# Other byte offsets for TensorE's two operands: split weights at 144 and 16 modulo 256, the stream as a run of high and a run of low halves

## What is computed

```python
qkv = xn @ w_qkv                      # 2048 x 6144
...
    return o.reshape(b, s, A_V_WIDTH) @ w_o
...
def _conv_ffn(xn, w_up, conv_w, conv_b, w_down):
    up = xn @ w_up                    # 2048 x 11264
    ...
    return (jax.nn.silu(g) * u) @ w_down
...
kv = _rmsnorm(h, kv_norm_g) @ b_w_kv  # 2048 x 4096
```

## Time and profile before

| what | value |
|---|---|
| runs | 2692.2, 2692.35, 2693.52 us |
| median | 2692.35 us |
| profiled execution, its own time | 2691.99 us |
| its span (first to last instruction) | 2689.8 us |
| TensorE (PE) busy | 2679.5 us |
| VectorE (DVE) busy | 1977.5 us |
| ScalarE (ACT) busy | 1197.8 us |
| data moved | 528.18 MB, 196 GB/s |

### The profile page before, as it was taken

One profiled execution on the slowest core, in us unless ns is written; L12 is line 12 of the kernel. 1 busy time (PEld: TensorE's weight loads), 2 busy tenths in 40 slices (PEclk: granted clock), 3 DMA queues, 4 the chain that ended last, 5 costly groups with the idle time before them and its releaser, 6 DMA issues.

```text
span 2689.8 us, 44167 instructions
## 1 busy us (share of the span) xinstructions
PE 2679.5 (100%) x15336; PEld 2348.9 (87%) x15336; DVE 1977.5 (74%) x2594; ACT 1197.8 (45%) x1533; POOL 5.7 (0%) x12
## 2 busy tenths in 40 slices
PE   9999999999999999999999999999999999999999
PEld 7888888888888888888888888888888888888888
DVE  6747577777777788667787776699878876688865
ACT  2004354555555444444444443366544444444443
POOL 0000000000000000000000000000000000000000
PEclk9999999999999999999999999999999999999999
DMA  9986665555556666666666666644566666666664
GB/s 342 366 278 191 205 192 191 165 174 163 160 164 196 188 195 190 198 190 195 189 194 188 196 200 190 188 157 140 181 188 195 196 191 192 192 190 195 196 202 155
DMA packets 705780, 528.18 MB, mean 196 GB/s; under 512 B 32221, under 2 KB 694559, under 8 KB 705439
## 3 DMA queue, kind: packets, MB, share of 16 engines
q1 hardware_dynamic: 701872, 523.73, 63.9%
q10 hardware_dynamic: 3823, 3.31, 0.4%
HBM read 523.80 MB, written 2.10 MB: 196 GB/s over the span
## 4 chain that ended last, share of the span: by engine, by line
PE 97%; DVE 2%; ACT 1%; issue 0%; DMA 0%; DVEq 0%; SPq 0%; ACTq 0%
PE acc L707 80%; PE acc L845 3%; PE acc L1039 2%; PE acc L833 2%; PE turned L845 2%; PE sums L845 2%; PE mixed L960 1%; PE sums L1191 1%; DVE pro_ada L1915 0%; DVE wr L1841 0%; PE scores L1184 0%; PE sums L745 0%; PE mixed L961 0%; PE sums L916 0%; PE scores L946 0%
## 5 line engine op out<-in xcount | busy, mean ns | idle before, releaser
L707 PE MATMUL acc<-stream,wr 128*128 128x512 f32 (+1 forms) x7680 | 1328.4, 333 | 0.3 <-DVE wr L1841 0.3
L707 PEld LDWEIGHTS acc<-stream,wr 128*128 128x128 f32 x7680 | 1159.1, 188 | 156.0 <-issue 3.8
L1841 DVE TENSOR_TENSOR wr<-raw,wr 128x1024 fp32r<-128x1024 f32 x832 | 998.5, 1222 | 318.2 <-ACT wr L1367 308.6
L1367 ACT ACTIVATE wr<-raw 128x1024 fp32r<-128x1024 f32 x832 | 871.1, 1058 | 693.8 <-PE acc L707 678.1
L707 PE MATMUL acc<-ys,wr 128*128 128x512 f32 (+1 forms) x4264 | 732.4, 332 | 1.0 <-DVE wr L1841 0.9
L707 PEld LDWEIGHTS acc<-ys,wr 128*128 128x128 f32 x4264 | 642.7, 188 | 85.3 <-DVE wr L1841 1.5
L707 PE MATMUL acc<-wr,stream 128*128 128x512 f32 (+1 forms) x1024 | 182.7, 338 | 0.0
L707 PEld LDWEIGHTS acc<-wr,stream 128*128 128x128 f32 x1024 | 157.0, 188 | 22.5 <-issue 0.5
L1725 ACT ACTIVATE ffn_cv<-ffn_cv 128x256 f32<-128x256 f32 x88 | 36.9, 419 | 245.4 <-DVE ffn_cv L2459 245.4
L1851 DVE TENSOR_REDUCE ffn_ug<-acc 128x512 f32<-128x1024 f32 x88 | 107.8, 1225 | 35.3 <-PE acc L707 35.3
L1874 DVE TENSOR_TENSOR ys<-tmp,ys 128x256 f32 (+3 forms) x108 | 51.2, 474 | 76.0 <-ACT ys L1373 73.4
(11 more groups left out here) (334 smaller groups left out, 1546.1 us busy)
## 6 DMA issues: line engine op xcount, KB each, us to landing
raw<-in_ffn_w_up SPq DMA_DIRECT2D x704, 256.0 KB
raw<-in_ffn_w_down SPq DMA_DIRECT2D x160, 512.0 KB
raw<-in_a_w_qkv SPq DMA_DIRECT2D x96, 512.0 KB
raw<-in_b_w_kv SPq DMA_DIRECT2D x64, 512.0 KB
aring<-in_w_ada SPq DMA_DIRECT2D x96, 256.0 KB, 6.6
w<-in_w_in SPq DMA_DIRECT2D x48, 512.0 KB
raw<-in_w_ada SPq DMA_DIRECT2D x32, 512.0 KB, 5.1
raw<-in_w_out SPq DMA_DIRECT2D x32, 512.0 KB
```

Of the source, the lines that this page charges most:

```text
L707: mm = pe.matmul(*ops, start=first and ops is wide, stop=last and ops is wide)
L1367: f(half_of(0, s), raw[:, s, :], ACT.Copy)\
L1841: tt(half_of(1, s), raw[:, s, :], half_of(0, s), ALU.subtract).then_inc(T.unit_split[s].sem, 1)
```

## The change

Three layouts are changed; no instruction is added, removed or moved.

- `wr`: WEIGHTS_SHIFT goes from 4 to 36 elements and HALF_PAIR from 2100 to 2080. The highs lie at 144 and the lows at 144 + 8320 = 16 modulo 256. SLOT_PAIR stays 4224 elements.
- `stream`: no longer high and low side by side tile for tile. All 16 high halves form one run, at 80 modulo 256, and all 16 low halves another, LOWS_SHIFT = 96 bytes further modulo 256, at 176. The tile is 192 bytes longer, so what is allocated behind it (`ssq`, `rx`, `kpe`, `ones_r`, `tri_r` and others) moves by 192 bytes.
- `ys` keeps its layout, high and low both at 80; only its view gains a dimension for the half.

All other lines of the diff are that extra dimension: `xs[:, k, :]` becomes `xs[:, k, :, :]`, and a range of columns becomes an index of the half.

```diff
-HALF_PAIR = 2 * UK * 256 + 52
-WEIGHTS_SHIFT = 4
-SLOT_PAIR = -(-2 * HALF_PAIR // 64) * 64
+LOWS_SHIFT = 96
+HALF_PAIR = 2 * UK * 256 + 32
+WEIGHTS_SHIFT = 36
+SLOT_PAIR = -(-(WEIGHTS_SHIFT + 2 * HALF_PAIR) // 64) * 64
...
-        stream = sb("stream", [KT * 2 * TOK + 2 * MOVING_SHIFT // 4], F32R)
-        xs_at = nc.sbuf_base - KT * 2 * TOK * 4 - 2 * MOVING_SHIFT
...
-        xs = moving_tiles(stream, KT)
+        run = KT * TOK + LOWS_SHIFT // 4
+        stream = sb("stream", [2 * run + 2 * MOVING_SHIFT // 4], F32R)
+        xs_at = nc.sbuf_base - 2 * run * 4 - 2 * MOVING_SHIFT
+
+
+        xs = stream[:, MOVING_SHIFT // 4:MOVING_SHIFT // 4 + 2 * run].rearrange("p (h r) -> p h r", h=2)[:, :, 0:KT * TOK]\
+            .rearrange("p h (k n) -> p k h n", k=KT)
...
                         if tokens_out:
-                            wide = (a[:, j, :], x[:, cols], both_halves)
-                            short = (a[:, j, 0:256], x[:, 256 + j * P:256 + j * P + P], high)
+                            wide = (a[:, j, :], x[:, 0, cols], both_halves)
+                            short = (a[:, j, 0:256], x[:, 1, cols], high)
                         else:
                             wide = (a[:, j, :], high[:, cols], x)
-                            short = (a[:, j, 0:256], low[:, cols], x[:, 0:TOK])
+                            short = (a[:, j, 0:256], low[:, cols], x[:, 0, :])
```

More of the change, by code:

```diff
@@ L360, in program @@
         begin_at("stream_gap", TILES_STEP)
-        stream = sb("stream", [KT * 2 * TOK + 2 * MOVING_SHIFT // 4], F32R)
-        xs_at = nc.sbuf_base - KT * 2 * TOK * 4 - 2 * MOVING_SHIFT
-        def moving_tiles(tensor, tiles):
-            return tensor[:, MOVING_SHIFT // 4:MOVING_SHIFT // 4 + tiles * 2 * TOK].rearrange("p (k n) -> p k n", k=tiles)
-        xs = moving_tiles(stream, KT)
+        run = KT * TOK + LOWS_SHIFT // 4
[3 more added lines that the diff above has]
+            .rearrange("p h (k n) -> p k h n", k=KT)
         xm = nc.alloc_sbuf_tensor_at("xm", [P, KT, TOK], F32, offset=xs_at)
@@ L371, in program @@
         gate_sum = nc.alloc_sbuf_tensor_at("gate_sum", [P, GATE_COLS], F32, offset=xs_at + KT * TOK * 4)
-        ys = moving_tiles(nc.alloc_sbuf_tensor_at("ys", [P, GROUP * 2 * TOK + 2 * MOVING_SHIFT // 4], F32R, offset=base), GROUP)
+        ys = nc.alloc_sbuf_tensor_at("ys", [P, GROUP * 2 * TOK + 2 * MOVING_SHIFT // 4], F32R, offset=base)[
+            :, MOVING_SHIFT // 4:MOVING_SHIFT // 4 + GROUP * 2 * TOK].rearrange("p (k h n) -> p k h n", k=GROUP, h=2)
         class Overlay:
@@ L730, in rows_pair @@
                         high, low = [half_of(part, s)[:, (k - k0) * 256:(k - k0 + 1) * 256] for part in range(2)]
-                        x_high, x_low = [right(k)[:, part * TOK + j * P:part * TOK + (j + 1) * P] for part in range(2)]
+                        x_high, x_low = [right(k)[:, part, j * P:(j + 1) * P] for part in range(2)]
                         out, last = a[:, j, 0:256], k == blocks - 1
@@ L1094, in woven_product @@
                 T.lo_out.n += KT // 2
-                ready, right = T.lo_out.n, lambda k: ys[:, k, :]
+                ready, right = T.lo_out.n, lambda k: ys[:, k, :, :]
                 pe.wait_ge(T.lo_out.sem, ready - 2)
@@ L1157, in two_pairs @@
                         if final and e == 1:
-                            rows_pair(lambda k: ys[:, k, :], blocks, after)
+                            rows_pair(lambda k: ys[:, k, :, :], blocks, after)
                         else:
-                            pair(lambda k: ys[:, k, :], blocks, before=gated if first and e == 0 else None, after=after)
+                            pair(lambda k: ys[:, k, :, :], blocks, before=gated if first and e == 0 else None, after=after)
                 per = dict(acc_read=2, **splits(2 * -(-blocks // UK)))
@@ L1228, in in_v @@
                             diff_out_sums()
-                    pair(lambda k: xs[:, k, :], before=None if live else normed, after=in_q)
-                    pair(lambda k: xs[:, k, :], before=lambda k: diff_sums(0) if k == UK + 1 else None, after=in_k)
-                    pair(lambda k: xs[:, k, :], after=in_v, tokens_out=True)
+                    pair(lambda k: xs[:, k, :, :], before=None if live else normed, after=in_q)
+                    pair(lambda k: xs[:, k, :, :], before=lambda k: diff_sums(0) if k == UK + 1 else None, after=in_k)
+                    pair(lambda k: xs[:, k, :, :], after=in_v, tokens_out=True)
             two_heads(True)
@@ L1261, in ffn @@
                     if g == 0:
-                        pair(lambda k: xs[:, k, :], before=normed_by, after=lambda n: stream_sums() if n == 1 else None)
-                        pair(lambda k: xs[:, k, :])
+                        pair(lambda k: xs[:, k, :, :], before=normed_by, after=lambda n: stream_sums() if n == 1 else None)
+                        pair(lambda k: xs[:, k, :, :])
                     with T.turns(pe, GROUP // 2 - (g == 0), **splits(2 * UK), acc_read=2):
                         for e in range(2):
-                            pair(lambda k: xs[:, k, :])
+                            pair(lambda k: xs[:, k, :, :])
                     residual_product(GROUP, stored=g == 1 and last, tiles=1)
@@ L1285, in _ @@
                     for e in range(2):
-                        pair(lambda k: xs[:, k, :], tokens_out=part == 1)
+                        pair(lambda k: xs[:, k, :, :], tokens_out=part == 1)
             for e in range(2):
-                pair(lambda k: xs[:, k, :], tokens_out=True)
+                pair(lambda k: xs[:, k, :, :], tokens_out=True)
             def stick_scores():
@@ L1330, in at_tile @@
                             stick_sums(0)
-                    pair(lambda k: xs[:, k, :], before=normed if first and e == 0 else at_tile, after=after)
+                    pair(lambda k: xs[:, k, :, :], before=normed if first and e == 0 else at_tile, after=after)
             two_query_pairs(True)
@@ L1389, in norm_splits @@
                     norms[0] += 1
-                    split((xs[:, 2 * g:2 * g + 2, 0:TOK], tmp[g % 2][:, :, :]))
+                    split((xs[:, 2 * g:2 * g + 2, 0, :], tmp[g % 2][:, :, :]))
             act.preload_act_table(ACT.Silu)
@@ L1535, in att_split @@
                 act.wait_ge(F.mixed_read.sem, 4 + it)
-                f(ys[:, 8 + 2 * it:10 + 2 * it, 0:TOK], tmp[0][:, :, :], ACT.Copy).then_inc(T.hi_out.sem, 1)
+                f(ys[:, 8 + 2 * it:10 + 2 * it, 0, :], tmp[0][:, :, :], ACT.Copy).then_inc(T.hi_out.sem, 1)
             def rnn_split(it):
-                split((ys[:, 2 * it:2 * it + 2, 0:TOK], S[1][:, :, :]))
+                split((ys[:, 2 * it:2 * it + 2, 0, :], S[1][:, :, :]))
             def att_gate(g):
@@ L1605, in two_pairs @@
                             f(sq[e][:, :, :], h[:, tiles, :], ACT.Square).then_inc(T.sq_ready.sem, 1)
-                            split((xs[:, tiles, 0:TOK], tmp[e][:, :, :]))
+                            split((xs[:, tiles, 0, :], tmp[e][:, :, :]))
                         if stored and first and e == 1:
@@ L1657, in diff_out_split @@
             def diff_out_split(tiles):
-                split((ys[:, tiles, 0:TOK], tmp[0][:, :, :]))
+                split((ys[:, tiles, 0, :], tmp[0][:, :, :]))
             def two_heads(first, i=None):
@@ L1725, in pair_of_tiles @@
                     f(cv[e][:, :], cv[e][:, :], ACT.Silu).then_inc(T.for_dve.sem, 1)
-                    split((ys[:, tile, 0:TOK], tmp[e][:, 0:1, :]))
+                    split((ys[:, tile, 0, :], tmp[e][:, 0:1, :]))
                 for g in range(2):
@@ L1873, in lo @@
                 dve.wait_ge(*T.hi_out.next())
-                tt(to[:, :, TOK:2 * TOK], src, to[:, :, 0:TOK], ALU.subtract).then_inc(*T.lo_out.one())
+                tt(to[:, :, 1, :], src, to[:, :, 0, :], ALU.subtract).then_inc(*T.lo_out.one())
             def norm(value, splits=()):
@@ L1887, in norm @@
                             own(T.split_me)
-                        lo(xs[:, 2 * g - 2:2 * g, :], tmp[(g - 1) % 2][:, :, :])
+                        lo(xs[:, 2 * g - 2:2 * g, :, :], tmp[(g - 1) % 2][:, :, :])
                     split_units(g in splits)
@@ L2227, in att_lo @@
             def att_lo(it):
-                lo(ys[:, 8 + 2 * it:10 + 2 * it, :], tmp[0][:, :, :])
+                lo(ys[:, 8 + 2 * it:10 + 2 * it, :, :], tmp[0][:, :, :])
             def rnn_gate(i):
@@ L2243, in rnn_lo @@
                 own(T.split_me)
-                lo(ys[:, 2 * i:2 * i + 2, :], S[1][:, :, :])
+                lo(ys[:, 2 * i:2 * i + 2, :, :], S[1][:, :, :])
             F.scores_ready.n, F.scores_read.n = 8, 8
@@ L2328, in two_pairs @@
                             w.then_inc(*T.squares_summed.one())
-                            lo(xs[:, tiles, :], tmp[e][:, :, :])
+                            lo(xs[:, tiles, :, :], tmp[e][:, :, :])
                 two_pairs(True)
@@ L2391, in diff_out_lo @@
                 own(T.split_me)
```

(4 more changed lines are left out.)

## The result

| | before | after |
|---|---|---|
| median | 2692.82 us | 2732.92 us |
| profiled execution, span | 2689.8 us | 2730.7 us |
| line of the matmuls, on `stream` (3840 pairs) | 1328.4 us | 1370.2 us |
| on `ys` (2132 pairs) | 732.4 us | 732.4 us |
| roles changed (512 pairs) | 182.7 us | 181.8 us |

Both medians are of four runs (2692.35, the number that the prediction started from, was that of the first three). The ratio of the runs is 1.0149, with a 95% interval of 1.0135 to 1.0162. One run of the changed kernel took 3575.59 us at a mean granted clock of 0.71; it stands outside the ratio.

What follows compares the result with a forecast made beforehand. The prediction took TensorE's pace from one matmul to the next as the bound. All terms were 0 except 3 us gained with changed roles: 2691.99 - 3 = 2689.0 us, forecast 2689 us, range 2662 to 2735 us.

Steps and rivals of the forecast that it cites:

- The term of +25 us: Usual form, 5972 short matmuls: 4.2 ns each if the distance between both operands decides; the forecast took 0.
- `rows_pair` itself: Its 132 matmuls, all distances changed to 64 and 192: at most 0.6 us, taken as 0.
- the term for the wide matmul of the usual form: Low weights loaded from 16, second 256 columns on `stream` from 176: taken as 0.
- The bound from above: Usual form, both matmuls together: 6.5 to 10.9 ns for each of 5972 pairs, +39 to +65 us.
- 580 matmuls in the window: Sign in the stretch 860 to 960 us: 580 or fewer means the distance decides, a pair at 344.9 ns or more.
- The forecast's case: Moving operand's place decides: usual form unchanged, a little back where roles are changed; 2689 us, chance 0.33.
- The rival, that the distance decides: Weights at 144 slow the usual form's short matmul: 2717 us, or 2731 to 2757 if the wide pays too; chance 0.30.
- The changed roles: 512 pairs with weights moving against activations: 3 us gained, at most 3.3 to 5.6 us, at worst nothing.
- The rival of no effect: The role alone makes the three paces and the offsets do nothing: 2692 us, chance 0.10.
- The faster rival: New offsets avoid part of a 15.6 ns read collision per usual-form pair: priced at 2662 us, chance 0.27.

Runs made afterwards that it cites:

- the one with `stream` at distance 64: The kernel before with both weight halves at 16, `stream` at 80 (distance 64) and `ys` at 208 (distance 192): 2736.83 us.

## Why the prediction failed

**What held.** TensorE's own pace was the bound and the only place at which the change could act; the idle time before the line stayed at 1 us or less, and ScalarE and VectorE took the new offsets without effect on it (871.1 and 998.5 us of work became 870.5 and 1000.7 us). The short matmul of the usual form with its weights at 144 costs nothing by itself: `ys` is at 732.4 us as before, and `stream` is back at 1328.3 us once the lows are at 80. The term of +25 us, taken from `rows_pair`, was rightly not taken. `rows_pair` itself kept its time, 15.9 us from its first start to its last in both kernels, as put.

**The step that failed** is the term for the wide matmul of the usual form. I wrote "I take 0, since the moving operand begins at 80 as in the fast rows", and called the second 256 columns at 176 something that no row has. It was the one moving operand of the usual form that went to an offset of which the trace had no row, and I gave it the price of its first half. It measured 41.8 us on 3840 pairs, 10.9 ns a pair, about 7 ns in the step of the wide matmul and 4 ns in that of the short one behind it, for which I had also taken 0. The bound from above had the same 10.9 ns, and the range, 2662 to 2735 us, held the 2732.92 us; both are luck. The bound was the difference to products with other roles and was meant for all 5972 pairs, and the upper end of the range came from a small cost on both tiles (2731 us), not from a large one on `stream` alone. The likeliest value was on the wrong side. (A small slip beside it: 580 matmuls in the window are 344.8 ns a pair, not 344.9; the count was 569.)

**The reason behind it** failed as well. The forecast's case was that the place of the moving operand decides. The kernel shifted as a whole by 64 bytes has other places for everything and the same groups to 0.1 us, so places alone decide nothing. The rival, that the distance decides, came out on the right side with the wrong mechanism: it put the cost on the short matmul by its distance of 192, on both tiles, and `ys` paid nothing; and no distance by itself is fast. What the runs show in its place is that the pace depends on the weights' and the activations' offsets together: the low halves at 176 cost 41.9 us with the weights at 144 and 16, 4.7 us with the weights at 16 and 224, and in the usual form the weights' move costs nothing with the lows at 80.

**The changed roles.** I took a gain of 3 us and measured 0.9. The weights' move alone lost 2.0 us there, which I had excluded with "at worst nothing"; the lows' move gave 2.9.

**The rival of no effect** is refuted by 40 us: equal instructions differ by up to 357.9 - 345.9 = 12.0 ns a pair by offsets alone. The rule of the Trainium skill that the prediction weighed ("TensorE: Matmul & The Clock Gate", section "Step-by-step: what each phase is for") is that loading the next weights takes nothing from the running matmul. These runs do not agree with the forecast of no effect that follows from it, since in the usual form the weights' offsets change the pace; they do not show where the two reads meet.

**The faster rival** found no support: the usual form's group is 1328.2 to 1328.4 us in three layouts (before, the weights alone, the lows back at 80) and never less in any of the twelve.

**What stays open** is how the reads meet. A rule that gives the pace from the four offsets was not found: with the weights at 16 and 224 and the highs at 80, lows at 80, 176 and 48 give 1328.4, 1333.1 and 1373.4 us; with 144 and 16, lows at 80, 128, 16 and 176 give 1328.3, 1357.2, 1367.5 and 1370.2 us, and both halves at 176 give 1365.1 us. That weight loads are the other party is inferred from the effect of the weights' offsets; no run leaves the loads out, and the record of a load lasts 188 ns in the slow layout and in the fast one. Offsets modulo 256 are how this document counts, and whether a larger modulus matters was not tried. A smaller one is not enough: modulo 128 the run with the lows back at 80 and the one with `stream` at distance 64 are alike, and they took 1328.3 and 1351.7 us. Most multiples of 16 and all offsets between them were left out, so a pace under the 340 ns of the undisturbed stretches is not excluded.

## What to carry to other kernels

Where TensorE is busy all the time and nobody is waited for, divide a group's busy time by its matmuls and compare groups of the same shape, type and roles: a difference at one clock can be a matter of where the operands lie, and here 10.9 ns a pair on `stream` was 1.5% of the kernel. Treat the offsets of all operands of a repeating sequence as one setting, and measure it as a whole. An operand, or half of one, for which the trace has no row at its new offset should get the whole bound of the unknown, not the price of its neighbour.

## What the runs showed of the hardware

Two things were not expected. Moving all operands together by 64 bytes changed no group by more than 0.1 us, so for that shift the effect is relative, and it repeats closely. And it carries over: on `stream` the short matmul, whose own operands and whose loaded weights lie in the same places, takes 117.8 ns to the next start instead of 113.6 ns when only the low halves that the matmul ahead of it reads lie at 176 instead of 80.
